# Router logits from unnormalised rows, experts' gates ahead of their downs, and the last weights and rows in halves

## The reference

```
x = x + mixed @ w_out
h = x * rsqrt(mean(x*x) + eps) * norm_ffn              # RMS norm
lg = h @ w_router_group + b;  group = the largest of 4
le = h @ w_router_expert + b; the two largest of the 4 experts in that group, softmax weights
for each chosen expert e: y_e = (silu(h @ gate[e]) * (h @ up[e])) @ down[e]
x = x + p_group * sum of weight_e * y_e
y = x * rsqrt(mean(x*x) + eps) * final_norm
```

## Time and profile before

| | |
|---|---|
| runs | 919.81 us median of 3 (917.28 to 924.47) |
| profiled execution | 914.95 us |
| its span | 913.1 us, 1.85 less |
| TensorE busy | 774.1 us (85% of the span) |
| VectorE, ScalarE, GpSimd busy | 278.2, 151.4, 64.1 us |
| mean granted clock of TensorE | 0.922 |
| bytes moved by DMA | 189.90 MB, mean 208 GB/s |

### The profile page before, as it was taken

How to read it: one execution, slowest core, us unless ns; L and a number is a source line. 1 busy time by engine, 2 the same in 40 slices (tenths; PEclk the granted TensorE clock), 3 DMA queues, 4 the chain that set the end, 5 groups by cost and what they waited for, 6 DMA issues and landing times. The chain is left out here.

```text
span 913.1 us, 10617 instructions
## 1 busy us (share of the span) xinstructions
PE 774.1 (85%) x4441; PEld 421.5 (46%) x4441; DVE 278.2 (30%) x702; ACT 151.4 (17%) x347; POOL 64.1 (7%) x97
## 2 busy tenths in 40 slices
PE   7999999889884989998897899999799787877760
PEld 3544577654552566555654435455333332332220
DVE  2150134568262442164216441135111110110004
ACT  3112122102331301140113110120000000000012
POOL 3102000003111000000001010002100000000002
PEclk9999999889997799999998879999899989988985
DMA  8956525505624200042204337409599999999934
GB/s 275 345 155 198 155 92 184 196 24 180 265 77 176 73 1 1 1 167 110 93 1 144 122 122 276 185 26 412 184 413 423 425 422 418 427 421 421 420 133 155
DMA packets 48830, 189.90 MB, mean 208 GB/s; under 512 B 5110, under 2 KB 5347, under 8 KB 44682
## 3 DMA queue, kind: packets, MB, share of 16 engines
q1 hardware_dynamic: 38922, 155.54, 43.8%
q0 software_dynamic: 9856, 33.63, 11.1%
HBM read 175.47 MB, written 17.88 MB: 212 GB/s over the span
## 5 line engine op out<-in xcount | busy, mean ns | idle before, releaser
L1148 PE MATMUL PS<-ring,arena 128*64 128x512 f32 x384 | 93.1, 643 | 20.8 <-issue 20.8
L1446 ACT ACTIVATE arena<-PS 128x512 f32<-128x512 f32 (+7 forms) x142 | 58.9, 441 | 268.5 <-PE PS L933 73.7
L864 PE MATMUL PS<-ring,hT 128*128 128x512 f32 x192 | 92.5, 630 | 0.4 <-ACT ring L1446 0.4
L562 PE MATMUL PS<-ring,hT 128*128 128x512 f32 x192 | 86.1, 605 | 0.0
L1148 PEld LDWEIGHTS PS<-ring,arena 128*64 128x64 f32 x384 | 32.9, 148 | 80.3 <-issue 80.3
L864 PEld LDWEIGHTS PS<-ring,hT 128*128 128x128 f32 x192 | 37.2, 202 | 43.8 <-issue 43.1
L562 PEld LDWEIGHTS PS<-ring,hT 128*128 128x128 f32 x192 | 36.4, 193 | 45.1 <-issue 45.0
L1446 ACT ACTIVATE brT<-PS 128x256 f32<-128x256 f32 (+2 forms) x39 | 16.3, 418 | 227.2 <-PE PS L1148 191.4
L652 PE MATMUL PS<-hT,ring 128*128 128x288 f32 x192 | 52.5, 431 | 0.0
L2419 DVE SCALAR_TENSOR_TENSOR brT<-brT,PS 128x256 f32<-128x256 f32 x16 | 6.7, 421 | 142.3 <-ACT brT L1446 142.3
L1173 PE MATMUL PS<-ring,brT 128*64 128x512 f32 x192 | 42.5, 594 | 4.6 <-ACT brT L1446 2.6
(11 more groups left out here) (361 smaller groups left out, 913.0 us busy)
## 6 DMA issues: line engine op xcount, KB each, us to landing
ring<-in_w_in SPq DMA_DIRECT2D x15, 2048.0 KB, 10.8
ring<-in_w_exp_gate SPq DMA_DIRECT2D x12, 2048.0 KB, 25.4
ring<-in_w_exp_up SPq DMA_DIRECT2D x12, 2048.0 KB, 24.1
ring<-in_w_exp_down SPq DMA_DIRECT2D x12, 2048.0 KB, 28.5
arena<-in_w_exp_down SPq DMA_DIRECT2D x4, 2048.0 KB, 21.8
arena<-in_w_exp_gate SPq DMA_DIRECT2D x4, 2048.0 KB, 27.7
arena<-in_w_exp_up SPq DMA_DIRECT2D x4, 2048.0 KB, 27.5
moe_in<-in_table SPq DMA_DIRECT2D x2, 2048.0 KB, 13.1
```

What stands on the lines that cost most here:

```text
L562: ins = pe.matmul(o[0:n, :], src[:, k, t0:t0 + n], unit(name)[:, 512 * k:512 * k + 512], start=(k == 0), stop=(k == KD - 1))
L864: ins = pe.matmul(PS[:, bg, :], hT[:, k, t0:t0 + n], wg_(k), start=(k == 0), stop=(k == KD - 1))
L1148: ins = pe.matmul(o[64 * hf:64 * hf + 64, :], hg[:, k, 64 * e:64 * e + 64], w[:, :, 512 * k + 256 * hf:512 * k + 256 * hf + 256], start=(k ...
L1446: return act.activation(o, i, f, **kw)
```

## The change

- **Router.** The logits are made from the unnormalised rows: TensorE turns `x2` itself (`turn_x2`, into `x2T`, with the gain from a new piece of `vecT`, loaded by SP at the start), and the row scale `rst` is multiplied in when VectorE reads the logits (`stt(... rst ..., brb, mult, add)`). Projection, turns and logits are woven: projection of tile 0, tile 2, turns of 0, first half of tile 1, turns of 2, logits of 0, second half of tile 1, turn of 1, logits of 2, turn of 1, logits of 1. The fillers between the turns (4) go, those after the ranking become 15 (12). The scaled rows `h2p` are written by ScalarE, and POOL waits for them ahead of `sid`. The third and fourth weight pairs wait for `("out", 1), 1`, now the last projection.
- **Experts.** A group is gate and up of all four, with turns between, then down of pair 0 and of pair 1. `G_PAIRS` follows. Activations get four places (`actT`).
- **Last weights.** The last down pair is loaded as four pieces: the first 512 columns of both experts (semaphore `d_half`), then the second 512 columns of both. TensorE waits for each half by itself.
- **Rows.** The first two reads of sorted rows are issued by SP, behind the fourth weight pair, when all six scatters are done (POOL before). The very last results are written by SP in two halves of 256 KB (POOL before, 512 KB whole).
- **The end.** Gathers, adds and output go by tiles 2, 0, 1 (`LAST_ORDER`); the norm of tile 2 comes ahead of the adds of tile 1.

```diff
+    OUT_ORDER = ((0, 0), (0, 1), (2, 0), (2, 1), (1, 0), (1, 1))
+    LAST_ORDER = (2, 0, 1)
...
-    G_PAIRS = [("gu", 0), ("gu", 1), ("d", 0), ("gu", 2), ("gu", 3), ("d", 1)]
+    G_PAIRS = [("gu", 0), ("gu", 1), ("gu", 2), ("gu", 3), ("d", 0), ("d", 1)]
...
+        turn_mixed(0, 1)
+        project_out(0, 0)
+        turn_mixed(1, 1)
+        turn_mixed(2, 1)
+        project_out(0, 1)
+        project_out(2, 0)
+        project_out(2, 1)
+        turn_x2(0, 0)
+        turn_x2(0, 1)
+        project_out(1, 0)
+        turn_x2(2, 0)
+        turn_x2(2, 1)
         pe.wait_ge(sg("wr_in"), 32)
         lg = use("lg", 1)
...
+        logits(0)
+        project_out(1, 1)
+        turn_x2(1, 0)
+        logits(2)
+        turn_x2(1, 1)
+        logits(1).then_inc(full[1], 1)
         keep_busy(4)
...
-        keep_busy(12)
+        keep_busy(15)
...
+            for e in range(EG):
+                gate_up(e, p, g)
+                if e == 1 and g < G - 1:
+                    turn_slots(0, p, g + 1)
+                if e == 2:
+                    turn_act(0, p, g)
+                    turn_act(1, p, g)
+                if e == 3 and g < G - 1:
+                    turn_slots(1, p, g + 1)
+            turn_act(2, p, g)
+            down(0, p, g)
+            turn_act(3, p, g)
+            down(1, p, g)
...
+            for nn in range(2):
+                if (g, pr_, nn) == (G - 1, 1, 0):
+                    pe.wait_ge(sg("d_half"), 32 * (p + 1))
+                else:
+                    for x in range(2):
+                        pe.wait_ge(*gready("d", 2 * pr_ + x, p, g))
...
                 elif s_ == 6:
-                    sp.wait_ge(*filled((("out", 1), 2)))
+                    sp.wait_ge(*filled((("out", 1), 1)))
...
+                    if q == 6 * G - 1:
+                        sp.dma_start(dst[:, :, 0:512], src[:, :, 0:512]).then_inc(sg("d_half"), 16)
+                    else:
+                        sp.dma_start(dst, src).then_inc(ring_full[gslot(kd_, ex, g)], 16)
+                if q == NPAIR - 1:
+                    sp.wait_ge(sg("x_out"), 96 * (p + 1))
+                    for pr_ in range(2):
+                        sp.dma_start(xg[pr_], pair_rows(xrows, pr_, 0)).then_inc(sg(f"xf{pr_}"), 16)
...
+            for nn in range(2):
+                sp.wait_ge(*moved("dn", 2 + nn, p, G - 1))
+                sp.dma_start(pair_rows(zrows, 1, G - 1)[:, 512 * nn:512 * nn + 512],
+                             outp[1][:, 512 * nn:512 * nn + 512]).then_inc(sg("z_last"), 16)
...
+        pool.wait_ge(sg("h2p"), 3)
         pool.wait_ge(sg("sid"), 1)
...
-            ins = tt(LG[0:n, t, :], bank_of("lg")[0:n, 20 * t:20 * t + 20], brb[0:n, :], ALU.add)
+            ins = stt(LG[0:n, t, :], bank_of("lg")[0:n, 20 * t:20 * t + 20], rst[0:n, t:t + 1], brb[0:n, :],
+                      ALU.mult, ALU.add)
...
+        add_rows(2, "last", 1, dstep)
+        add_rows(0, "last", 1, dstep)
         dve.wait_ge(sg("gfin_in"), 16)
+        final_norm(2)
+        add_rows(1, "last", 1, dstep)
+        final_norm(0)
+        final_norm(1)
```

More of the change, by code:

```diff
@@ L1085, in keep_busy, with logits @@
+        def logits(t):
+            t0, n = TILES[t]
+            for k in range(KD):
+                if k % 4 == 0:
+                    pe.wait_ge(*taken(("x2T", t, k // 4)))
+                ins = pe.matmul(lg[0:n, 20 * t:20 * t + 20], x2T[:, k, t0:t0 + n], wr[:, k, :],
+                                start=(k == 0), stop=(k == KD - 1))
+            return ins
         def keep_busy(n):
+            pe.wait_ge(free[3], count[3])
             for _ in range(n):
                 pe.matmul(PS[:, 3, :], ident, cst[:, 0:512], start=True, stop=True)
+        turn_mixed(0, 1)
@@ new lines, in group, with gate_up @@
+            for e in range(EG):
[11 more added lines that the diff above has]
+            down(1, p, g)
+        def gate_up(e, p, g):
+            pe.wait_ge(*gready("g", e, p, g))
+            pe.wait_ge(*gready("u", e, p, g))
+            pe.wait_ge(*gtaken("gu", e, p, g))
+            o = gbank("gu", e)
+            w = gunits(gslot("g", e, g))
+            for k in range(KD):
+                if e % 2 == 0 and k % 4 == 0:
+                    pe.wait_ge(*moved("xT", e + k // 4, p, g))
+                for hf in range(2):
+                    ins = pe.matmul(o[64 * hf:64 * hf + 64, :], hg[:, k, 64 * e:64 * e + 64],
+                                    w[:, :, 512 * k + 256 * hf:512 * k + 256 * hf + 256],
+                                    start=(k == 0), stop=(k == KD - 1))
+            ins.then_inc(gfull("gu", e), 1)
@@ new lines, in turn_act, with down @@
+        def turn_act(e, p, g):
+            pe.wait_ge(sg("act"), (4 * p + g) * 4 + (e + 1))
+            pe.wait_ge(*gtaken("aT", e, p, g))
+            o = gbank("aT", e)
+            for c in range(2):
+                ins = pe.transpose(o[:, 128 * c:128 * c + 128], actb[:, e % 2, 128 * c:128 * c + 128], ident)
+            ins.then_inc(gfull("aT", e), 1)
+        def down(pr_, p, g):
+            for e in (2 * pr_, 2 * pr_ + 1):
+                pe.wait_ge(*moved("aT", e, p, g))
+            for nn in range(2):
[4 more added lines that the diff above has]
+                        pe.wait_ge(*gready("d", 2 * pr_ + x, p, g))
+                pe.wait_ge(*gtaken("dn", 2 * pr_ + nn, p, g))
+                o = gbank("dn", 2 * pr_ + nn)
+                for c in range(4):
+                    hf, cc = c // 2, c % 2
+                    for x in range(2):
+                        w = gunit("d", 2 * pr_ + x, g)[:, D * c + 512 * nn:D * c + 512 * nn + 512]
+                        ins = pe.matmul(o[64 * x:64 * x + 64, :],
+                                        actT[2 * pr_ + x][:, 128 * cc + 64 * hf:128 * cc + 64 * hf + 64], w,
+                                        start=(c == 0), stop=(c == 3))
+                ins.then_inc(gfull("dn", 2 * pr_ + nn), 1)
@@ L1410, in slots_group @@
                     read_slots(pr_, p, g + 2)
+            for pr_ in range(2):
+                if (g, pr_) == (G - 1, 1):
+                    continue
                 for nn in range(2):
```

299 lines of the change are left out of this document (132 added, 167 removed).

## The result

The changed kernel takes **914.88 us** (median of 20 runs, 908.07 to 920.92), the kernel before, on the same chip, 920.17 us (20 runs, 914.57 to 925.91). The ratio is 0.9944, 95% interval [0.9917, 0.9971]: about 5 us, or half a per cent, faster. The profiled execution has a span of 909.8 us, 3.3 less than the 913.1 of before.

A forecast was written before the change was run, and what follows sets the result against it. DMA engines, never free from 660.5 to 873.3 us at 420 GB/s, were taken as the bound. Terms +0.3 - 0.8 - 1.2 - 3.4 - 1.3 - 1.6 = -8.0 us gave 911.5 us, range 905.5 to 917.5.

The forecast's parts named there:

- the rival of low clock at the end: Last downs: both run at low clock after idle waits, tail 20.0 us, gain 3.5 in all, 916.3; chance 0.15.
- the slow rival: Last down pair: halves with 2 KB rows load slowly, second half at +15.4, 3.5 us worse, 915.3; chance 0.08.
- T0: End of the last projection matmul: 615.6 us predicted for 612.9, later by turns and logits moved ahead of it.
- The lead is eaten: Router to first sorted rows: slots known 4.6 us sooner, but only 0.8 us gained at the first turn.
- half the rate beside the weights: Scatter of routed rows: 2.36 MB at 203 GB/s beside the weights takes 11.6 us, to 640.7, seen at 642.6.
- the reads are held behind the weights on SP's queue: First reads of sorted rows: they wait for SP's weights until 645.0 and are seen at 647.2, against 648.0.
- weights still moving at the first read: Sign of being right: weights still moving when the first sorted rows are read.
- The rival built on it: First reads on SP's queue not held behind weights: rows at 645.3, 1.9 us more gain, 909.9; chance 0.15.
- The seventh write: End of the weight stream: a 0.52 MB result write no longer precedes the 22nd pair, -1.2 us on its landing.
- From the landing of the 22nd pair: TensorE's work after that landing: 15.5 us for 18.95, -3.4, including 0.3 for a chance of low clock.
- The halves: Last down pair loaded in halves: second in at +10.5, hidden with 1.1 us to spare, worth 0.9 to 1.9.
- Last rows and gathers: End of the kernel: last write in halves -1.3 us, gathers and adds with small tile first -1.6 us.

The follow-up runs named there:

- reads_pool: Changed kernel with only the first two reads of sorted rows put back on POOL's queue, no pair held; ratio to the kernel before 0.9924.
- old_order: Changed kernel with the group order of gates and downs put back to that of before; ratio to the kernel before 1.0014.
- norm_last: Changed kernel with the small tile's final norm behind the adds of tile 1 on VectorE; ratio to the kernel before 0.9956.
- hold_pool: Changed kernel with the fourth weight pair held behind the scattered rows, first reads issued by POOL at the same moment; ratio to the kernel before 0.9953.
- late_slots: Changed kernel with 20 more small VectorE operations ahead of the slot numbers, slots known 4.1 us later; one run, 915.0 us.

## Why the prediction was right, and where its steps were off

911.5 us was forecast with 905.5 to 917.5; 914.88 was measured, ratio 0.9944 where the forecast said 0.991. The time lies in the range, and a change within 1% had the largest chance. The size was over-estimated: the sum was -8.0 us; the two profiled executions differ by -3.3 and the ratio says -5.2 [-7.6, -2.7], which leaves -8.0 out. Of the cases, the forecast's mechanism came, and with it, in the profiled execution, half of the rival of low clock at the end (one of the two downs, total -3.3 where the rival had -3.5). Three figures of the prediction do not follow from its own terms. The bounds of the terms add up to -3.4 and -12.5 us, not to -2.6 and -12.8. The chances give 0.15 + 0.55 / 3 = 0.33 for faster by over 1%, not 0.38, and 0.60 for within it. And the 10.8 us of the slow rival is a median of 15 loads, not the time of a lone one.

**T0.** Predicted 615.6, was 615.37 (614.7 without the drift of the part before). The clock loss of 1.7 us ahead of the projection went altogether (granted 1.00 in 580 to 584) where I took half. The logits' sum at T0 + 3.6 for 4.0, the slots at 626.35 for 627.5.

**The lead is eaten.** Predicted 0.8 of 4.6 us, measured 0.5 of 5.8, and shown twice: holding the fourth pair gives 7.8 us at the first turn, and making the slots 4.1 later costs 0.7. The sum of bytes was the right argument. The step inside it was wrong: I gave the scatter half the rate beside the weights. By that the rows were in at 640.7 and the weights at 645.0. In the trace it is the other way round: the weights are in at 641.1, 25.7 us after T0 as in the kernel before, and the rows are seen at 644.92. With one 4 KB packet of rows for one 16 KB packet of weights the rows get a fifth, not half. The first turn came out right because both orders end with the same bytes, and in that it is luck. That the reads are held behind the weights on SP's queue did not come up, because the weights were already in (weights still moving at the first read was one of my signs of being right; it did not come); reads_pool shows that the queue made no difference here. The rival built on it was therefore empty, not wrong.

**The stream.** 420 GB/s again; no rate was lost. The seventh write no longer ahead of the 22nd pair: -0.8 for -1.2 by the first buffer free, and 1.0 between old_order and the new order.

**From the landing of the 22nd pair.** Predicted 15.5, measured 18.0, the largest miss (2.5 of the 4.7 us between the sum and the executions). The step that failed is the clock, on both sides of the difference. I put 0.3 for a chance of low clock after the change, though I had the wait, and the row of before with 9.52 for the same cause: over seven executions the term is 1.3 us, and the rest, 15.1 at full clock, is as summed. And I counted the 9.52 of before as something that the change takes away, when it is a draw too: at full clock before takes 18.95 - 2.43 = 16.5 (old_order: 16.5), so at equal clock the term is -1.4, not -3.4.

**The halves.** Worth 1.7 us for 0.9 to 1.9, and no wait at the second half, whose last piece landed 10.4 us after the first downs started, for 10.5 predicted. The rule on 1 MiB (the Trainium skill, "DMA: Bandwidth & Descriptors", section Bandwidth) would have put the second half 1.2 us late, at 12.8; the trace does not agree: beside that 10.4, in all executions with halves the last 32 matmuls run unbroken in 7.09 us, behind a wait of 0.52 for ScalarE.

**Last rows and gathers.** -0.9 for -1.3: the write of 256 KB and the wake-ups took 5.8 from the last matmul to the gather where I had 5.4. Gather to end 21.3 for 20.65: the adds of tile 1 start at 12.7 for 12.3 (12.9 in norm_last, where they wait for the rows), and the last operations take 8.6 for 8.35. The write in halves and the order of the gathers were not tested by themselves; their shares are read from the two profiled executions alone.

## What to carry to other kernels

When a result comes sooner, look at what is queued between it and its consumer before counting the gain: here 4.2 MB of weights, in at 641.1 and first used by the fourth gate and up at 675.21, stood beside 2.4 MB of rows that TensorE was waiting for, and moving that one pair behind the rows was worth about as much again as the whole change (0.9872 against 0.9944, 7.0 us from T0 to the end). Hold back as much as the gap has room for, and no more; and send what is urgent ahead of the bulk in the same queue, since beside it in another queue it gets packet for packet, here 4 KB against 16, and may still come last. A matmul group that follows a wait of about 3 us should be priced at its mean over both clocks, in the kernel before as well as after, not at the one that a single trace shows.

## What the hardware showed that I had not expected

- 1 MB of reads issued on POOL's queue within half a microsecond of a 4.2 MB pair on SP's queue landed after 10.8 and 14.0 us (median 12.4), the second with the last of the pair (13.8); alone they took 3.9. The Trainium skill ("DMA: Bandwidth & Descriptors", section Queues, rings and completion order) says that each DMA engine goes round the queues that have work, packet by packet. The trace agrees with turns of one packet each: 183 packets against 179 where SP's are of 16 KB and POOL's of 4, and 94 against 97 where both are of 4 KB, and only there were the bytes shared evenly. By an even share of the bytes (an estimate from the 368 GB/s of that stretch of hold_pool) the reads would have been in after about 6 us, so the share here was not even in bytes.
- The same wait of 2.9 us ahead of the same 32 matmuls is followed by 10.04, 9.97, 8.76, 8.48 or 7.09 us. What decides between them stays open: late_slots and the changed kernel have the same work and waits (2.94 and 2.96) ahead of it.
- Six scatters of 0.5 MB or less with nothing beside them take 9.3 us from the first issue to the last landing, 7.3 of it POOL's issues. Below that, a sooner row needs fewer or cheaper issues, not more bandwidth.
